# A hybrid decoder layer on one Trainium2 core: gate and up weights in 4 MB pieces over a ring of ten places, float32 gather

## What is computed

```python
logits = (xt @ router_w + router_b).astype(jnp.float32)      # 32 experts
top_val, top_idx = lax.top_k(logits, TOP_K)                  # 4 of them per token
gates = jax.nn.softmax(top_val, axis=-1).astype(h.dtype)
...
gu = xb @ w_gate_up[e] + b_gate_up[e]                        # 1024 x 2048
g, u = gu[:, :D_FF], gu[:, D_FF:]
g = jnp.minimum(g, SWIGLU_LIMIT)
u = jnp.clip(u, -SWIGLU_LIMIT, SWIGLU_LIMIT)
act = (u + 1) * (g * jax.nn.sigmoid(SWIGLU_ALPHA * g))
return (act @ w_down[e] + b_down[e]) * wb[:, None]           # 1024 x 1024
```

## Time and profile before

| | before |
|---|---|
| time, median of 3 | 1149.9 us |
| profiled execution: its own time | 1151.61 us |
| its span (first to last instruction) | 1149.7 us |
| PE busy / DVE / ACT | 93% / 22% / 15% |
| PE clock, mean | 0.99 |
| moved from memory | 430.55 MB, 375 GB/s over the span |
| chain that ended last | PE 56%, DMA 39% |

### The profile page before, as it was taken

How to read it: one execution, slowest core, us unless ns; L and a number is a source line. 1 busy time by engine, 2 the same in 40 slices (tenths; PEclk the granted TensorE clock), 3 DMA queues, 4 the chain that set the end, 5 groups by cost and what they waited for, 6 DMA issues and landing times.

```text
span 1149.7 us, 15140 instructions
## 1 busy us (share of the span) xinstructions
PE 1063.8 (93%) x6271; PEld 476.3 (41%) x6271; DVE 250.0 (22%) x656; ACT 170.3 (15%) x341; POOL 6.8 (1%) x17
## 2 busy tenths in 40 slices
PE   7999989799999999999999999999999999999996
PEld 5788876533333333333333333333333333333332
DVE  1588742721111111111111111111111111111101
ACT  3453340411100000000000000000000000000000
POOL 1000000000000000000000000000000000000000
PEclk9999999899999999999999999999999999999998
DMA  9843275599999999999999999999999999999995
GB/s 289 301 126 112 74 291 222 182 428 416 427 429 429 428 429 428 428 428 429 428 428 429 429 429 429 427 429 428 382 422 429 429 429 428 429 429 429 428 428 219
DMA packets 52643, 431.90 MB, mean 376 GB/s; under 512 B 5075, under 2 KB 23838, under 8 KB 28174
## 3 DMA queue, kind: packets, MB, share of 16 engines
q1 hardware_dynamic: 51984, 431.04, 90.7%
q0 software_dynamic: 272, 0.43, 0.2%
q10 hardware_dynamic: 366, 0.15, 0.1%
HBM read 430.55 MB, written 1.05 MB: 375 GB/s over the span
## 4 chain that ended last, share of the span: by engine, by line
PE 56%; DMA 39%; ACT 2%; DVE 1%; issue 1%; SPq 1%; ACTq 0%; DVEq 0%
DMA arena<-in_w_down 29%; PE psum L781 17%; PE psum L804 14%; DMA arena<-in_w_gate_up 10%; PE psum L589 5%; PE psum L504 4%; PE psum L814 3%; PE psum L642 2%; PE psum L680 2%; PE psum L751 2%; PE psum L766 1%; ACT arena L1044 1%; PE psum L792 1%; PE psum L759 1%; PE psum L580 0%
## 5 line engine op out<-in xcount | busy, mean ns | idle before, releaser
L781 PE MATMUL psum<-arena 128*64 128x512 f32 x2048 | 448.7, 594 | 9.5 <-DMA arena<-in_w_gate_up 9.0
L804 PE MATMUL psum<-arena 128*64 128x512 f32 x1024 | 233.1, 604 | 51.3 <-DMA arena<-in_w_down 37.1
L781 PEld LDWEIGHTS psum<-arena 128*64 128x64 f32 x2048 | 144.2, 137 | 311.6 <-issue 292.3
L1345 DVE TENSOR_SCALAR arena<-psum 128x512 f32<-128x512 f32 x32 | 22.1, 691 | 760.7 <-PE psum L781 749.9
L804 PEld LDWEIGHTS psum<-arena 128*64 128x64 f32 x1024 | 71.4, 138 | 190.9 <-issue 137.2
L1032 ACT COPY arena<-psum 128x512 f32<-128x512 f32 x32 | 18.7, 585 | 490.8 <-PE psum L751 490.8
L814 PE MATMUL psum<-arena 64*128 64x512 f32 x256 | 63.7, 615 | 0.7 <-ACT arena L1048 0.7
L751 PEld LDWEIGHTS psum<-arena 128*128 128x128 bf16 x1536 | 48.4, 98 | 29.2 <-issue 29.2
L589 PE MATMUL psum<-arena 128*128 128x256 f32 x256 | 58.8, 381 | 0.3 <-ACT arena L963 0.3
L1048 ACT COPY arena<-psum 128x512 f32<-128x512 f32 x32 | 18.7, 585 | 265.9 <-PE psum L804 265.9
L751 PE MATMUL psum<-arena 128*128 128x64 bf16 x1536 | 52.2, 194 | 4.0 <-DVE arena L1278 4.0
(11 more groups left out here) (218 smaller groups left out, 497.0 us busy)
## 6 DMA issues: line engine op xcount, KB each, us to landing
arena<-in_w_gate_up SPq DMA_DIRECT2D x128, 2048.0 KB, 26.2
arena<-in_w_down SPq DMA_DIRECT2D x63, 2048.0 KB, 21.9
arena<-in_w_in SPq DMA_DIRECT2D x9, 1024.0 KB, 6.1
arena<-in_w_in SPq DMA_DIRECT2D x8, 512.0 KB, 9.0
arena<-in_w_out SPq DMA_DIRECT2D x1, 4096.0 KB, 17.2
arena<-in_w_o_mla SPq DMA_DIRECT2D x1, 2048.0 KB, 10.0
arena<-in_conv_pw_w SPq DMA_DIRECT2D x1, 2048.0 KB, 15.9
arena<-in_w_down SPq DMA_DIRECT2D x4, 512.0 KB, 21.0
```

Of the source, the lines that this page charges most:

```text
L781: last = mm(b[64 * half:64 * half + 64, :], xe[i][:, k, :], gu[i][c][:, j, o + half * 512:o + half * 512 + 512], start=(k == 0 and bias_la ...
L804: last = mm(Y[64 * c:64 * c + 64, :], aT[:, j, 64 * h:64 * h + 64], dn[h][:, j, c * 512:(c + 1) * 512], start=(h == 0 and j == 0), stop=(h ...
L1345: ts(g_s, G, LIMIT, None, ALU.min).then_inc(S.g_ready, 1)
```

## The change

1. **Pieces and places.** GC, GR go from 4, 2 to 2, 4: a gate/up piece is 4 MiB in 32 KB runs and takes two adjacent places of a ring of ten 2 MiB places; down pieces stay 2 MiB. One semaphore `used` counts all pieces, and SP loads gate/up and down in plain order. Weights of the first expert are all loaded after attention.
2. **Gather in float32.** `xn3` is gone. The gather takes the un-normed state `h1` itself, float32, reordered in its access pattern (a step of GR = 4 floats between the columns of the stationary operand); `ph` is float32 and carries the row's norm factor. DVE takes the gathered rows out (L1383), multiplied by the norm's weight, in the midst of `activations`; ACT did it before.
3. **Tail of the router.** The residual is added by DVE after the output projection, which now goes in five parts with transposes and router steps between; the residual is put into banks 0 to 3 afterwards (L700), beside the first expert's gather, which is done in two halves (L732).
4. **Layer norm.** DVE adds the four channel tiles first, so each column sum is one product and not four.
5. **Start.** Three and five products on zeros (`busy`) ahead of the first transposes.
6. The item loop is written out for five experts with three sets of side buffers.

```diff
-GC, GR = 4, 2
+GC, GR = 2, 4
 DC, DR = 2, 4
+PER, UNITS, RING10 = GC + DC, 6, 10
+ROUND = 5
+SIDE = [0, 1, 0, 1, 2]
...
+        CHUNK = 4096
+        unit_at = [A0 + CHUNK * c for c in range(4)] + [D0, D0 + CHUNK] + [B0 + CHUNK * c for c in range(4)]
...
-        ph = [words(at + 64 * i, 64).bitcast(BF16).rearrange("p (t s) -> p t s", t=2) for i in range(2)]; at += 128
+        ph = [grid(at + 128 * i, 2, SLOTS) for i in range(2)]; at += 256
...
+            for p in range(GC):
+                load(0, p, 0)
+            sp.wait_ge(S.ymix_ready, 4)
+            load(0, GC, 0)
             sp.wait_ge(S.mix_ready, 4)
...
+            load(0, GC + 1, 0)
+            load(1, 0, 1)
+            sp.wait_ge(S.h1_ready, 5)
+            load(1, 1, 1)
+
+            with sp.Fori(0, (E - 2) // ROUND) as it:
+                for m in range(PER + GC, PER + GC + ROUND * PER):
+                    e, p = m // PER, m % PER
+                    sp.wait_ge(S.used, ROUND * PER * it + free_before(e, p))
+                    load(ROUND * it + e, p, e)
...
+            busy(6, 3, SEQ)
             pe.wait_ge(in_ident, 16)
...
+            busy(6, 5, SEQ)
...
+            pe.wait_ge(S.lnsum_ready, 1)
+            filled("lnmu", mm(fill("lnmu")[:, 0:SEQ], ones, lnsum[:, 0, :], start=True, stop=True))
...
-                    for t in range(2):
-                        for part in range(3):
-                            last = mm(X[:, k * SLOTS:(k + 1) * SLOTS], xn3[:, t, part, k * P:(k + 1) * P],
-                                      ph[i][:, t, :], start=(t == 0 and part == 0), stop=(t == 1 and part == 2))
+                        last = mm(X[:, k * SLOTS:(k + 1) * SLOTS], row_order(h1[:, t, :])[:, k // GR, k % GR, :],
+                                  ph[i][:, t, :], start=(t == 0), stop=(t == 1))
...
+            def rows_out(i, first, last):
+                n = last - first
+                return tt(xe[i][:, first:last, :], X[:, first * SLOTS:last * SLOTS].rearrange("p (k s) -> p k s", k=n),
+                          fnw[:, first:last].unsqueeze(2).to_broadcast([P, n, SLOTS]), ALU.mult)
...
                 ts(a_s, U, LIMIT, -LIMIT, ALU.min, ALU.max).then_inc(S.a_step, 1)
...
+                if after is not None:
+                    dve.wait_ge(S.gathered, n + 2)
+                    rows_out(after, 0, KD).then_inc(S.xe_ready, 1)
                 dve.wait_ge(S.g_ready, n + 1)
```

More of the change, by code:

```diff
@@ L458, in _ @@
                                ).then_inc(in_bias, 16)
+            with nc.allow_non_contiguous_dma(reason="the norm's weight in the order of the experts' rows"):
+                pool.dma_start(fnw.rearrange("p (c j) -> p c j", j=GR),
+                               a["ffn_norm_w"][0].rearrange("(c p j) -> p c j", c=GC, j=GR)).then_inc(in_bias, 16)
             pool.wait_ge(S.ymix_ready, 4)
@@ L475, in filled, with busy @@
                 ins.then_inc(bank_full[plan[job][0]], 1)
+            def busy(bank, times, n):
+                for _ in range(times):
+                    mm(psum[:, bank, 0:n], idle[:, 0:P], idle[:, 0:n], start=True, stop=True)
+            pe.wait_ge(S.cols_clear, 3)
+            busy(6, 3, SEQ)
             pe.wait_ge(in_ident, 16)
@@ new lines, in turn_state, with router @@
+            def turn_state(part):
+                t, c, n = part
+                pe.wait_ge(S.h1_ready, OUT_PARTS.index(part) + 1)
+                b = fill(("ht",) + part)
+                for i in range(n // P):
+                    at = c + i * P
+                    last = nc.tensor.transpose(b[:, i * P:(i + 1) * P], h1[:, t, at:at + P], ident)
+                filled(("ht",) + part, last)
+            small_bank = psum[:, 5, :]
+            LG, RANK = (0, E), 2 * E
+            def router(t, first, last):
+                if first == 0:
+                    pe.wait_ge(S.router_ready, 1)
+                    fill(("lg", t))
+                for k in range(first, last):
+                    ins = mm(small_bank[:, LG[t]:LG[t] + E], hT[:, k, :], rwt[:, k, :], start=(t == 0 and k == 0),
+                             stop=(k == KD - 1), skip_group_check=True)
+                if last == KD:
+                    filled(("lg", t), ins)
@@ L732, in down_biases @@
                 pe.wait_ge(S.gateT_ready, 1)
-                pe.wait_ge(in_bias, 48)
-                for bank in range(4):
-                    free(bank)
+                pe.wait_ge(in_bias, 64)
                 for t in range(2):
@@ L793, in turn_act, with down @@
                 last.then_inc(S.aT_done, 1)
-            def down(n, loads, in_pieces=False):
+            def down(n, like, more=0, in_pieces=False):
                 pe.wait_ge(S.aT_ready, n + 1)
@@ L798, in down @@
                     if h == 0 or not in_pieces:
-                        pe.wait_ge(in_dn[h], loads[h])
+                        pe.wait_ge(in_piece[like % ROUND][GC + h], 16 * (like // ROUND + 1) + more)
+                    w = place(like, GC + h)
                     for j in range(DR):
@@ L816, in scatter, with item @@
                 last.then_inc(S.scattered, 1)
-            def item(n, i, gu_loads, dn_loads, final=False):
-                gate_up(n, i, gu_loads)
+            def item(n, i, before, after, like, more=0, final=False):
+                gate_up(n, i, like, more)
                 if not final:
-                    gather(n + 1, 1 - i)
-                scatter(n - 1, 1 - i)
+                    gather(n + 1, after)
+                scatter(n - 1, before)
                 if not final:
-                    turn(n + 1, 1 - i)
+                    turn(n + 1, after)
                 turn_act(n)
-                down(n, (dn_loads, dn_loads), in_pieces=final)
-            free(6)
-            pe.wait_ge(S.split_ready, 2)
-            gather(0, 0)
+                down(n, like, more, in_pieces=final)
+            free(4)
+            free(5)
+            gate_up(0, SIDE[-1], 0, bias_last=True)
+            b = fill("cnt")[:, 0:E]
+            mm(b, ones, maskt[:, 0, :], start=True, stop=False)
+            filled("cnt", mm(b, ones, maskt[:, 1, :], start=False, stop=True))
+            turn(0, SIDE[-1])
             pe.wait_ge(S.gate_ready, 2)
```

587 lines of the change are left out of this document (299 added, 288 removed).

## The result

| | before | after |
|---|---|---|
| median of the runs beside each other | 1150.05 us (4 runs, 1149.17 to 1150.66) | 1348.6 us (4 runs, 1346.81 to 1349.63) |
| ratio after/before, 95% interval | | 1.1725 (1.1705 to 1.1746) |
| span of the profiled execution | 1149.7 us | 1347.2 us |
| TensorE's granted clock, mean over the span | 0.99 | 0.904 |

The forecast was 1172 us, with a range to 1186. The direction was right, the size was off by 177 us: the gather costs twice what was put down for it (7.66 us an expert against 3.84), and something that was not in the forecast at all goes with it.

The account below looks back on a forecast made before the run. The prediction took the weight stream to bound the kernel before and PE after the change. Its terms: 217.2 to the first gate/up + 35.5 to the second + 30 x 29.54 + 33.1 = 1172.0 us, range 1152 to 1186.

Parts of the forecast that it names:

- What bounds the kernel before: Whole kernel before the change: the weight stream sets the end, and up to 1.4 us more per expert on PE is free.
- I take 0.12 us a record: Gather in each expert: 32 float32 records at 0.12 us, paced by stepped weight loads, 3.84 us in all.
- the dear bound of 0.177: Gather in each expert: upper bound of 0.177 us a record, with 70 ns on top for the step, 5.66 us in all.
- One expert = 25.7 + G: PE time per expert after the change: 25.7 us plus the gather's time G; with G = 3.84, 29.54 us.
- Start: Kernel's first records: products on zeros bring PE to full pace early and save 2.4 us, bounds 0 and 3.
- First gate/up at 217.2: Work ahead of the experts: first gate/up comes at 217.2 us instead of 229.55, range 215 to 221.
- To the second gate/up 35.5: First to second gate/up: 32.6 as before, plus 2.3 for the longer gather and 0.6 for gate transposes, 35.5 us.
- The last expert 33.1: Last expert to the span's end: 13.88 gate/up, 4.31 to down, 7.09 down and 7.8 after, together 33.1 us.
- The stream meanwhile: Weight loads after the change: the stream alone would end near 1136 us, so it does not bind.
- The rivals: Whole kernel: free step 1159 us (0.25), dear step about 1228 (0.10), faster stream-bound (0.10), 32 KB runs cut into 16 KB packets (main case).
- the dear step: Rival on the gather: the step adds 70 ns to each record, gather 5.66 us, total about 1228 us; chance 0.10.

## Why the prediction was wrong, by its own steps

- **What bounds the kernel before**: right. The tripled gather shows that 1.3 to 1.4 us an expert are free, and that what lies beyond is paid in full.
- **"I take 0.12 us a record"**: this is the step that failed. Measured 0.239, and outside the dear bound of 0.177 too. The bound was set from L792, a transpose, whose *length* rose by 70 ns with the step; the gather's load rose by 138 (330 against 192), and its pace by 123 (239 against 116). Two things in the earlier trace rows could have warned. L792 is a transpose and makes one record, where a float32 product makes two, and its pace was read from only four loads, the first of which starts 0.27 us before its own products (360.68 against 360.95), where 32 in a row leave nothing to run ahead of. That this is why four loads looked cheap was not tested. A row of another operation showed a direction, and it was taken for the upper bound too. 32 x (0.239 - 0.12) = 3.8 us an expert, 115 us.
- **The clock**: missing altogether, and the second step that failed. The forecast kept scatter and turn at their rows of before. Behind stepped loads the scatter takes 3.04 to 3.72 us in place of 1.92. 34.78 - 29.23 (without the step) = 5.55 us an expert, of which the gather is 3.94 and this is 1.61, 48 us over thirty.
- **One expert = 25.7 + G**: right as a number where the clock holds. With G = 3.72 it gives 29.42, measured 29.23; the 0.2 is the chain from the gather's end to down, 3.53 us (480.90 to 484.43) where 3.7 was put. The path was another one: the forecast had DVE's three operations there, and the chain of the run without the step goes through PE's own scatter, turn and turned activations and their copy on ACT, with DVE hidden beneath.
- **Start**: first block of L510 12.34 3.93 against 13.15 6.04, 2.9 us earlier at its end, 2.1 of it in the block itself, where 2.4 was forecast. With the layer norm and the residual products the output projection starts at 177.04 in the profiled run (175.37 in the run without the step), for a forecast of 175.85.
- **First gate/up at 217.2**: 222.41, and 217.00 without the step. Between these two 3.8 us are the first gather, 3.55 + 3.73 us in two halves against 1.73 and 1.78. The other 1.7 were there before it: 32 records of L641 took 8.25 us with a granted clock of 0.84, against 6.91 at full clock in the run without the step, though the two kernels do the same up to that point.
- **To the second gate/up 35.5**: 46.53, and 40.65 without the step. So 5 us of this miss have nothing to do with the step. In that run PE waits from 230.96 + 1.06 to 234.40 us, but for 0.39, for the activations' first half and for the gates' transposes and their copy on ACT. Then it does the gate-weighted biases (L761) in 5.87 us where before had 3.63, with a granted clock of 0.50 between 236 and 242 us. Before, nothing of the kind stands ahead of those products, and the clock is full.
- **The last expert 33.1**: 34.9 in the changed kernel and in the one without the step. Down takes 8.81 us there and not 7.09. The forecast saw 8.81 in the earlier trace rows and put it down to late weights. That reading was wrong: in the run without the step nothing is late and it is 8.81 again, with the clock at 0.51 for its first 3 us, behind 4.3 us in which PE waits for DVE and ACT and is busy for 2.6. The forecast's number was fair all the same. Behind the same wait nine of the thirteen traces have down at 7.11 us with the clock full, and four have 8.81 (both kernels, the one without the step, and the half gather with 16 KB runs).
- **The whole error**, span against span: 5.2 us to the first gate/up, 11.0 to the second, 30 x 5.24 = 157.2 in the thirty experts, 1.8 in the last, together 175.2 = 1347.2 - 1172.0.
- **The stream meanwhile**: right that it does not bind; 431 GB/s for 32 KB is as worked out. The stream alone gives 1142, not 1136. That larger pieces, freed as a whole, cost nothing holds only as long as PE sets the pace: in the two half gathers they cost as much as the longer runs gave.
- **The rivals**: the dear step was the right one in kind, at 0.10, and its figure (1228) was still 120 us short. The run without the step (1172) lands on the forecast's number partly by luck: its experts, 29.27 us in the mean against 29.54, save 8 us, and the second gate/up and the last expert give 7 of them back.

What stays open: why the clock falls behind stepped loads. The runs exclude length by itself (7.29 us without the step keeps it full) and show that the step suffices at 3.93 us. A stepped gather has PE do less in a given time (a record per 239 ns where 116 are possible), so a low pace and not the step as such may be what counts. The traces speak for that: the clock also falls where no load is stepped and PE has stood still or been busy for only part of the time, to 0.54 behind a gap of the doubled gather and to 0.51 behind the wait of the last expert. But the same wait and the same eight stepped records bring it down in some cases and not in others. A gather without a step that is slowed in another way was not tried.

## What to carry to other kernels

Where float32 weight loads set the pace, as in this gather, a stationary operand that is read with a step costs by how many columns share 16 bytes: with 8 bytes from column to column almost nothing, with 16 bytes twice the time at full clock. Longer steps were not tried. When a layout is changed for the DMA's sake, look at which matmul operand inherits the step, and give the step to a copy, or to the partitions, before you trade it for a per cent of bandwidth. And bound an unseen cost from a row of the same operation in the same repetition; a longer instruction elsewhere shows a direction, not an upper end.

## What the runs showed of the hardware

- Gathers with 128x128 float32 stationary operands, time over records: 116 ns without a step, 122 with 8 bytes, 239 to 245 with 16 bytes; from load to load 112, 118 and 233. The pace with 16 bytes does not hang on the clock (233 ns at a granted clock of 1.00 and of 0.50), the pace without a step does (112 and 213).
- The granted clock stands at its lower level, 1.2 GHz, behind 16 or 32 stepped loads, though PE counts as busy all through; behind eight it did so in 6 of 30 experts. 64 records without a step left it at 2.4 GHz.
- The granted clock also falls behind 3 to 5 us in which PE is idle in whole or in part: to 0.54 behind such a gap of the doubled gather, and behind the last expert's wait (PE busy for 2.6 of 4.2 us) in four traces of thirteen.
- DMA runs of 8, 16 and 32 KB for the gate/up weights (16 KB for down in each): 424, 427 to 429 and 431 GB/s at a full queue.
- When the item loop grew by 80 float32 products a pass, the queue that carries instructions went from 17 packets to 69 over the kernel, and PE stood still for 3 to 5 us in each pass.
